# One weight quadrant of the gated feed-forward layer taken by a second level of Strassen: the upper right block of gate and up in a fused transformer layer

## The chip, the cores and the metric

The kernel runs on one core of a Trainium2 chip. The metric is the device time of one launch in microseconds; lower is better. The engines of the core are TensorE (PE, with its weight loads PEld), VectorE (DVE), ScalarE (ACT), GpSimd (POOL) and SyncE (SP), which only starts transfers here.

## The reference, cut to what matters

The program is a whole hybrid layer (latent attention, an RWKV branch, output projection, feed-forward) over 1024 prompt tokens and 32 sample tokens. The change touches its last part alone:

```
def layer_tail(x, attn, rw, attn_out_g, w_out, norm_ffn_g, w_gate, w_up, w_down):
    mix = jnp.concatenate([rmsnorm(attn, attn_out_g), rw], axis=-1)
    h = x + mix @ w_out
    u = rmsnorm(h, norm_ffn_g)
    return h + (jax.nn.silu(u @ w_gate) * (u @ w_up)) @ w_down
```

All is float32. The model width is 1024 (8 blocks of 128, `KD`), the hidden width 2816 (22 blocks, `FB`), and there are 1056 tokens (`TOK`).

## The kernel before, in words

The function is `tail`. Tokens lie along the free dimension; `uT` holds the normed input as 8 depth blocks by 1056 tokens. The products with gate and up are done by Strassen's scheme in Winograd's form with seven products: the weights are cut in two row blocks (output block `pair` and `pair + 11`) and two depth halves of four blocks (`KH`), the tokens in two halves of 528, and each half in two column quarters of 264 (`NW`). A **unit** is one matrix (gate or up) and one pair of output blocks: 22 units, even ones gate, odd ones up. A unit has two **steps**, one for each column quarter `nh`: 44 steps.

A step computes, in PSUM banks X, Y, Z, W (banks 0 to 3 in even steps, 4 to 7 in odd ones), in this order: X = A11·B11, Y = S2·T2, Z = S3·B12, W = S1·T1, and then on top of what the banks hold X += A12·B21, Z += A22·T4, W += S4·B22. Each product is four matmuls of 128x264, and each float32 matmul is two records in the trace, so a product is 8 records. Between them ScalarE copies the first content of X into `p1_`, and VectorE adds it through the others: `u2 = Y + P1` (line 2910), `u3 = Z + u2` (2912), `u3 = W + u3` (2914). The second product of X waits for the copy, that of Z for 2912, that of W for 2914. After these, VectorE finishes the four output quadrants. In gate steps (lines 2921 to 2938) it multiplies by the row factors `rb`, ScalarE takes a tanh, and VectorE writes (1 + tanh)·value into `hid`; in up steps (2940 to 2948) it multiplies `hid` by half the result. All are VectorE operations of 128x264; some read one operand from PSUM and one from SBUF, the others read both from SBUF (2921, 2927, 2928, 2933 to 2940, 2947, 2948).

GpSimd makes the four weight sums of each unit, 128x512 each (S1, S2, S3, S4; lines 2795, 2797, 2798, 2800), from the weights that SyncE loads into the two buffers `ab[0]` (gate) and `ab[1]` (up), 2 x 512 KB each unit. The load of a unit waits until the unit that used its buffer is through (line 2505).

After the units come eight steps of the down projection (`DOWN`) of the same form, with products of eleven matmuls and weight sums by GpSimd (lines 2805 to 2819); its token sums (`sums`, lines 2960 to 2966) are VectorE's. Its first step needs the first weights `Alo` (in the gate buffer) and `Ahi` (in the up buffer).

The order of all work on each engine is written out by hand; the engines meet by semaphores alone.

Of the kernel before, what the change touches and what calls it, by code (L numbers as in the profile page):

```python
# [11 lines left out]
P = 128  # L12
# [2397 lines left out]
def tail(nc, g, io, phase):  # L2410
# [26 lines left out]
    wa = [w[:, :, :] for w in g.wo] + slots[0:4]  # L2437
# [6 lines left out]
    p1_ = [sb(f"p1_{i}", [P, NW]) for i in range(2)]  # L2444
# [8 lines left out]
    sw = [w[:, 2 * KD * P:].rearrange("p (s k n) -> p s k n", s=3, k=KH) for w in wA]  # L2453

# [10 lines left out]
    names = """xr_in0 xr_in1 xr_in2 xr_in3 xr_in4 xr_in5 xr_in6 xr_in7 g_in hi_in5 hi_in6 hi_in7 in0 in1 in2 in3 lo_read u_hi1 zero ps_done end_done part_ok h_ok hc_ok sq_ok acc_ok ssq_ps ms_ok r_ok rb_ps rb_ok u_lo u_hi h_st  # L2465
# [7 lines left out]
    UNITS = 2 * FH  # L2473
    DOWN = [(nh, j) for nh in range(2) for j in range(KH)]

    @block.sync
    def _(sp):
# [34 lines left out]
        for u in range(2, UNITS):  # L2512
            sp.wait_ge(s["w_ps"], 2 * u - 2)
            load_unit(u)

        def rows(j):
            return io.w_down[j]

        for n, (nh, j) in enumerate(DOWN):
            sp.wait_ge(s["w_ps"], 2 * UNITS - 2)  # L2520
            if n:
# [3 lines left out]
            sp.dma_start(Alo[:, 0:FH], rows(j)[:, 0:FH]).then_inc(s["a11_in"], 16)  # L2525
            if n == 0:
                sp.dma_start(Alo[:, FH:], rows(j)[:, FH:]).then_inc(s["a12_in"], 16)
            sp.wait_ge(s["w_ps"], 2 * UNITS)
# [34 lines left out]
    def _(pe):  # L2563
# [53 lines left out]

        for u in range(UNITS):
            b = u % 2
            pe.wait_ge(s[f"w_in{b}"], 32 * (u // 2 + 1))  # L2620
            for nh in range(2):
                it, c = 2 * u + nh, slice(nh * NW, nh * NW + NW)
                X, Y, Z, W = (4 * (it % 2) + i for i in range(4))
                half = lambda t: (lambda k: t[:, k, c])
                left = lambda w: (lambda k: w[:, k, :])
                A11, A12, S3, A22 = (ab[b][:, a, KH * d:KH * d + KH] for a in range(2) for d in range(2))
                if it == 0:
                    pe.wait_ge(s["hc_ok"], KD - 2)
                    pe.wait_ge(s["u_lo"], KH)
                if it == 1:  # L2630
                    pe.wait_ge(s["h_ok"], 2 * KD)
                    pe.wait_ge(s["hc_ok"], KD)
                if it >= 2:
                    pe.wait_ge(s["x_done"], it - 1)
                product(X, left(A11), half(B11u), KH, "p1_ps")
                if it == 1:
                    row_factors()
                if it == 0:
                    pe.wait_ge(s["s1_ok"], 1)
                    pe.wait_ge(s["t1_ok"], 1)  # L2640
                    product(W, left(sw[b][:, 0]), half(T1u), KH, "p5_ps")
                pe.wait_ge(s["s2_ok"], u + 1)
                if it == 0:
                    pe.wait_ge(s["t2_ok"], 1)
                if it == 1:
                    pe.wait_ge(s["rb_ok"], 1)
                if it >= 2:
                    pe.wait_ge(s["y_done"], it - 1)
                product(Y, left(sw[b][:, 1]), half(T2u), KH, "p6_ps")
                pe.wait_ge(s["s3_ok"], u + 1)  # L2650
                if it == 0:
                    pe.wait_ge(s["t3_ok"], 1)
                if it == 1:
                    pe.wait_ge(s["rb_ok"], 2)
                if it >= 2:
                    pe.wait_ge(s["z_done"], it - 1)
                product(Z, left(S3), half(B12u), KH, "p7_ps")
                if it == 0:
                    pe.wait_ge(s["u_hi"], KH)
                else:  # L2660
                    pe.wait_ge(s["s1_ok"], u + 1)
                    if it == 1:
                        pe.wait_ge(s["rb_ok"], 3)
                    if it >= 2:
                        pe.wait_ge(s["w_done"], it - 1)
                    product(W, left(sw[b][:, 0]), half(T1u), KH, "p5_ps")
                pe.wait_ge(s["p1_ok"], it + 1)
                product(X, left(A12), half(B21u), KH, "x_ps", first=False)
                if it == 0:
                    pe.wait_ge(s["t4_ok"], 1)  # L2670
                pe.wait_ge(s["u3_ok"], it + 1)
                product(Z, left(A22), half(T4u), KH, "z_ps", first=False)
                pe.wait_ge(s["s4_ok"], u + 1)
                pe.wait_ge(s["c22_ok"], it + 1)
                product(W, left(sw[b][:, 2]), half(B22u), KH, "w_ps", first=False)
                if it == 0:
                    row_sums()

        for n, (nh, j) in enumerate(DOWN):
            X, Y, Z, W = (4 * (n % 2) + i for i in range(4))  # L2680
# [3 lines left out]
            left = lambda w: (lambda k: w[:, k, :])  # L2684
            pe.wait_ge(s["a11_in"], 16 * n + 16)
            if n == 0:
                pe.wait_ge(s["hid_ok"], 6 * UNITS)
            if n >= 2:
                pe.wait_ge(s["q_x"], n - 1)
            product(X, left(Alo[:, 0:FH]), lo0, FH, "q1_ps")  # L2690
# [34 lines left out]
    def _(act):  # L2725
# [26 lines left out]
        for u in range(UNITS):  # L2752
            for nh in range(2):
                it = 2 * u + nh
                X, Y, Z, W = (4 * (it % 2) + i for i in range(4))
                act.wait_ge(s["p1_ps"], it + 1)
                act.activation(p1_[it % 2][:, :], pb[X][:, 0:NW], ACT.Copy).then_inc(s["p1_ok"], 1)  # L2757
                if it == 0:
                    for last in (KD - 2, KD - 1):
                        squares(last)  # L2760
                if u % 2:
                    continue
                n = u + nh + 1
                act.wait_ge(s["c22_s"], n)
                act.activation(th[1], part[1][:, :], ACT.Tanh, scale=0.5).then_inc(s["th22"], 1)
                act.wait_ge(s["c11_ok"], n)
                act.activation(th[0], g11[:, :], ACT.Tanh, scale=0.5).then_inc(s["th11"], 1)
                act.wait_ge(s["c21_ok"], n)
                act.activation(th[2], part[2][:, :], ACT.Tanh, scale=0.5).then_inc(s["th21"], 1)
                act.wait_ge(s["c12_ok"], n)  # L2770
                act.activation(th[3], part[0][:, :], ACT.Tanh, scale=0.5).then_inc(s["th12"], 1)
        for n in range(len(DOWN)):
            act.wait_ge(s["q1_ps"], n + 1)
            if n >= 2:
                act.wait_ge(s["q_u2"], n - 1)
            act.activation(p1_[n % 2][:, :], pb[4 * (n % 2)][:, 0:NW], ACT.Copy).then_inc(s["q1_ok"], 1)  # L2776

    @block.gpsimd
    def _(pool):
# [7 lines left out]
        for u in range(UNITS):  # L2787
            if u == 2:
                pool.wait_ge(s["ms_ok"], 2)
                tt(row_ms[:, :], row_ms[:, :], minus_half, ALU.pow).then_inc(s["r_ok"], 1)  # L2790
            b = u % 2
            A11, A12, A21, A22 = (ab[b][:, a, KH * d:KH * d + KH] for a in range(2) for d in range(2))
            S1, S2, S4 = (sw[b][:, i] for i in range(3))
# [4 lines left out]
            tt(A21, A11, A21, ALU.subtract).then_inc(s["s3_ok"], 1)  # L2798
            pool.wait_ge(s["s2_ok"], u + 1)
            tt(S4, A12, S2, ALU.subtract).then_inc(s["s4_ok"], 1)  # L2800
        pool.wait_ge(s["w_ps"], 2 * UNITS)
        for n in range(len(DOWN)):
            pool.wait_ge(s["a11_in"], 16 * n + 16)
# [18 lines left out]
    def _(dve):  # L2822
# [77 lines left out]
        for u in range(UNITS):  # L2900
            pair = u // 2
            if u == 2:
                dve.wait_ge(s["h_st"], 16)
            for nh in range(2):
                it = 2 * u + nh
# [9 lines left out]
                if it == 0:  # L2915
                    row_means()
                    row_factors()
# [206 lines left out]
```

## Time and profile before

| | |
|---|---|
| median of 3 runs | 1805.3 us (1804.81 to 1805.52) |
| the profiled execution's own time | 1805.66 us |
| its span, first to last instruction | 1803.9 us |
| mean granted TensorE clock | 0.992 |
| PE busy | 1728.3 us, 96% of the span |
| DVE busy | 951.5 us, 53% |
| ACT busy | 414.0 us, 23% |
| POOL busy | 617.5 us, 34% |

The span is one profiled execution; what is added to it in the profiled execution's own time, 1.8 us, lies around the first and last instruction. Busy time of PE counts matmuls from issue to modelled end, so neighbours overlap; how fast they follow each other is read from the timeline or from the chain of work that ended last.

### The profile page before, as it was taken

The page shows a single profiled execution, that of the slowest core. Times are in us where ns is not written, and L with a number is a line of the kernel's source. Part 1 is how long each engine was busy: PE and PEld are TensorE (multiplying, and loading weights), DVE is VectorE, ACT ScalarE, POOL GpSimd, SP SyncE. Part 2 cuts the span into 40 slices and gives each one's busy share as a digit, 9 for nine tenths or more (in the row PEclk, how much of TensorE's full clock was granted, in tenths as well). Part 3 has the DMA queues.
Part 4 walks back from the last instruction along what each step waited for, and adds up shares of the span by engine and source line. Part 5 has one row for each costly group of instructions (what it writes and reads, how often), then busy time and mean ns, then how long its engine had stood idle before and what let it go on. Part 6 is the DMA issues. An engine that isn't in the chain of part 4 may idle for free.

```text
span 1803.9 us, 34817 instructions
## 1 busy us (share of the span) xinstructions
PE 1728.3 (96%) x14732; PEld 1309.8 (73%) x14732; DVE 951.5 (53%) x1758; ACT 414.0 (23%) x945; POOL 617.5 (34%) x431
## 2 busy tenths in 40 slices
PE   5899999999998996999999999999999999999998
PEld 4566666666665654666666888888888888888887
DVE  2757767767766675666435433444433345526322
ACT  2343333333334232556211001011110010000000
POOL 2654663663653552000150211222212221635332
PEclk9999999999999998999999999999999999999999
DMA  9443253243244312610052111011110112333431
GB/s 351 161 159 109 62 163 109 78 146 109 79 134 112 106 40 73 184 49 13 18 223 96 47 47 47 25 47 47 48 47 24 47 47 76 121 104 105 145 104 53
DMA packets 89008, 169.36 MB, mean 94 GB/s; under 512 B 29627, under 2 KB 62987, under 8 KB 84630
## 3 DMA queue, kind: packets, MB, share of 16 engines
q1 hardware_dynamic: 79510, 117.85, 20.5%
q10 hardware_dynamic: 9344, 49.29, 7.9%
q8 instruction: 118, 1.93, 0.4%
q14 instruction: 36, 0.29, 0.1%
HBM read 136.40 MB, written 23.04 MB: 88 GB/s over the span
## 4 chain that ended last, share of the span: by engine, by line
PE 49%; DVE 1%; issue 0%; POOL 0%; ACT 0%; DVEq 0%
PE psum L2613 45%; PE psum L2566 4%; DVE u_sum L2876 0%; DVE mixT L2877 0%; PE psum L2601 0%; POOL row_ms L2790 0%; DVE mixT L2850 0%; DVE hid L2847 0%; DVE rb L2896 0%; PE psum L2607 0%; DVE hid L2837 0%; DVE yout L2997 0%; DVE part L2946 0%; DVE part L2996 0%; DVE part L2912 0%
## 5 line engine op out<-in xcount | busy, mean ns | idle before, releaser
L2613 PE MATMUL psum<-mixT,wA 128*128 128x264 f32 x1408 | 335.2, 386 | 0.4 <-DVE mixT L2877 0.4
L2613 PEld LDWEIGHTS psum<-mixT,wA 128*128 128x128 f32 x1408 | 267.4, 190 | 46.4 <-issue 0.8
L2613 PE MATMUL psum<-u_sum,wA 128*128 128x264 f32 x1232 | 297.2, 386 | 2.3 <-DVE part L2912 1.5
L497 PE MATMUL psum<-wsl,xt 128*128 128x368 f32 (+2 forms) x1100 | 286.4, 451 | 8.8 <-DMA wsl<-in_w_in 5.5
L2613 PEld LDWEIGHTS psum<-u_sum,wA 128*128 128x128 f32 x1232 | 233.8, 190 | 43.0 <-issue 3.2
L497 PEld LDWEIGHTS psum<-wsl,xt 128*128 128x128 f32 (+1 forms) x1100 | 151.8, 172 | 91.9 <-issue 18.1
L2795 POOL TENSOR_TENSOR wA<-wA 128x512 f32<-128x512 f32 x22 | 29.4, 1337 | 392.4 <-DMA wA<-in_w_gate 197.1
L2613 PE MATMUL psum<-hid,wA 128*128 128x264 f32 x528 | 120.2, 386 | 2.1 <-DVE hid L2948 1.5
L2613 PEld LDWEIGHTS psum<-hid,wA 128*128 128x128 f32 x528 | 100.2, 190 | 19.9 <-issue 2.8
L2201 PE MATMUL psum<-kT,qT 104*128 104x346 f32 (+7 forms) x224 | 80.1, 477 | 12.5 <-DMA kT<-scratch_kT 9.1
L1539 POOL TENSOR_TENSOR Ls<-Lraw,con 128x512 f32<-128x512 f32 x45 | 48.8, 1093 | 97.1 <-ACT Lraw L1143 66.1
L2613 PE MATMUL psum<-mixT,u_sum 128*128 128x264 f32 x352 | 79.8, 386 | 0.0
L2757 ACT ACTIVATE p<-psum 128x264 f32<-128x264 f32 x44 | 17.1, 390 | 253.6 <-PE psum L2613 253.4
L2613 PEld LDWEIGHTS psum<-mixT,u_sum 128*128 128x128 f32 x352 | 66.8, 190 | 11.7 <-POOL u_sum L2815 0.3
L1505 POOL TENSOR_TENSOR st<-st,con 128x3 f32<-128x3 f32 (+1 forms) x18 | 50.7, 2816 | 60.6 <-DVE st L1702 31.3
L1143 ACT ACTIVATE proj<-psum,rstd 128x368 f32<-128x368 f32 (+1 forms) x72 | 36.9, 512 | 142.9 <-PE psum L497 142.3
L2367 DVE TENSOR_REDUCE part<-psum 128x1 f32<-128x347 f32 (+5 forms) x88 | 44.3, 523 | 43.1 <-PE psum L2201 42.1
L2289 ACT ACTIVATE pq<-psum,neg 128x346 f32<-128x346 f32 (+7 forms) x112 | 59.8, 542 | 27.6 <-DVE neg L2370 21.4
L2805 POOL TENSOR_TENSOR wA<-wA 128x1408 f32<-128x1408 f32 x8 | 25.5, 3182 | 112.1 <-DMA wA<-in_w_down 112.1
L2776 ACT ACTIVATE p<-psum 128x264 f32<-128x264 f32 x8 | 3.1, 391 | 255.0 <-PE psum L2613 255.0
L2910 DVE TENSOR_TENSOR part<-psum,p 128x264 f32<-128x264 f32 x44 | 19.0, 432 | 79.2 <-PE psum L2613 79.1
L2341 POOL COPY wide<-rec 128x256 f32<-128x256 f32 x16 | 6.4, 402 | 154.4 <-DVE rec L2380 154.4
(363 smaller groups left out, 2904.0 us busy)
## 6 DMA issues: line engine op xcount, KB each, us to landing
wsl<-in_w_in ACTq DMA_DIRECT2D x27, 1472.0 KB, 6.5
wA<-in_w_down SPq DMA_DIRECT2D x32, 704.0 KB, 4.2
wA<-in_w_gate SPq DMA_DIRECT2D x22, 512.0 KB, 4.3
wA<-in_w_up SPq DMA_DIRECT2D x22, 512.0 KB, 4.3
mixed<-proj SPq DMA_DIRECT2D x8, 784.0 KB
xt<-in_x_tiles SPq DMA_DIRECT2D x9, 512.0 KB, 5.1
wsl<-in_w_in SPq DMA_DIRECT2D x3, 1472.0 KB, 13.4
hid<-in_x_cols SPq DMA_DIRECT2D x8, 528.0 KB, 7.2
```

The lines of the kernel that those rows point to most:

```text
L497: return pe.matmul(out, lhsT, rhs, start=start, stop=stop)
L1143: copy = lambda out, in_, **k: act.activation(out, in_, ACT.Copy, **k)
L1505: tt(out, ms, c_("minus_half")[:, 0:n], ALU.pow).then_inc(s[ok], 1)
L1539: tt(Ls[i % 2][:, :, :], Lraw[:, :, :], bcast(c_("levels")[:, i * 64:(i + 1) * 64], 1, H), ALU.mult).then_inc(s["Ls_ok"], 1)
L2201: pe.matmul(pb[n % BANKS][:, 0:y - x], qT[b][0:ROWS, t * P:(t + 1) * P], kT[b][0:ROWS, x:y], start=True, stop=True).then_inc(s["s_ps"], 1)
L2289: act.activation(rows_of(a, t)[:, x:y], pb[n % BANKS][:, 0:y - x], ACT.Exp, bias=neg[:, i % RINGS:i % RINGS + 1], accum_out=sums[:, pair % ...
L2367: dve.tensor_reduce(part[:, r, u:u + 1], src, AX.X, ALU.max).then_inc(s["part_ok"], 1)
L2566: last = pe.matmul(pb[bank][:, 0:c.stop - c.start], w[:, k, :], g.mixT[:, first_k + k, c], start=start and k == 0, stop=stop and k == 3, s ...
L2613: ins = pe.matmul(pb[bank][:, 0:NW], left(k), right(k), start=first and k == 0, stop=k == depth - 1, skip_group_check=not first)
L2795: tt(S1, A21, A22, ALU.add).then_inc(s["s1_ok"], 1)
L2805: tt(Ahi[:, 0:FH], Alo[:, 0:FH], Ahi[:, 0:FH], ALU.subtract).then_inc(s["e3_ok"], 1)
L2910: named(tt(u2, Y, p1_[it % 2][:, :], ALU.add), "y_done", it + 1)
```

## The change

The product A12·B21 (upper right weight block, four depth blocks) is no longer part of the seven products of each step. A step of first level keeps six products; its first content of X is only copied. Two units (four steps) form a **double**: the two weight blocks A12 of the double's two units are taken as two row blocks, their four depth blocks as two halves of two (`DK`), the two column quarters of B21 as the two column blocks, and their product, the same that four first-level steps used to need, is done by a further step with seven products of two matmuls each (`second_level`). There are 11 doubles of 5 steps, 55 steps in all. The first double mixes gate and up of the last block pair; the others are two gate units, then two up units of the same two blocks, in turn.

The copies P1 of the four first-level steps are kept in four buffers until the second-level step adds its results to them: VectorE then has per double 17 operations in the second-level step of a gate double, 13 in that of an up double, 15 in the mixed one; a first-level step has 11 (gate) or 8 (up) where it had 13 or 9. GpSimd gets four sums of 128x256 per double, VectorE four sums of 128x528 once, after the second step. The weights are loaded in other pieces and at other moments: A11 with the second row block (256 and 512 KB) as before, but the second unit's only after the fourth step of the double before, and the A12 blocks (256 KB each) after its second-level step. GpSimd's order in a double is S1, S2, S3 of the first unit, S1, S2, S3 of the second, S4 of both, then the four small sums. At the start of the down projection the first weights come in three pieces, one of which (`Alo[:, KH:2*KH]`, which lies where A12 of the first unit is) is loaded only after the last step, and the matmuls of the first product are put in another order.

```
+    DOUBLES = [((0, FH - 1), (1, FH - 1))] + [((b, p), (b, p + 1)) for p in range(0, FH - 1, 2) for b in range(2)]
+    STEPS = [(d, j) for d in range(FH) for j in range(5)]
...
-        for u in range(2, UNITS):
-            sp.wait_ge(s["w_ps"], 2 * u - 2)
-            load_unit(u)
+        for d in range(1, FH):
+            sp.wait_ge(s["w_ps"], 5 * d - 3)
+            load_unit(2 * d)
+            sp.wait_ge(s["w_ps"], 5 * d - 1)
+            load_unit(2 * d + 1)
+            sp.wait_ge(s["w_ps"], 5 * d)
+            load_twelve(2 * d)
+            load_twelve(2 * d + 1)
...
         for n, (nh, j) in enumerate(DOWN):
-            sp.wait_ge(s["w_ps"], 2 * UNITS - 2)
+            if n == 0:
+                sp.wait_ge(s["w_ps"], N_STEPS - 3)
+                sp.dma_start(Alo[:, 0:KH], rows(j)[:, 0:KH]).then_inc(s["lo_in"], 16)
+                sp.dma_start(Alo[:, 2 * KH:FH], rows(j)[:, 2 * KH:FH]).then_inc(s["lo_in"], 16)
+                sp.dma_start(Alo[:, FH:], rows(j)[:, FH:]).then_inc(s["a12_in"], 16)
+                sp.wait_ge(s["w_ps"], N_STEPS)
+                sp.dma_start(Alo[:, KH:2 * KH], rows(j)[:, KH:2 * KH]).then_inc(s["a11_in"], 16)
...
-                product(X, left(A12), half(B21u), KH, "x_ps", first=False)
...
+        def second_level(it, d):
+            X, Y, Z, W = (4 * (it % 2) + i for i in range(4))
+            pe.wait_ge(s["p1_ok"], it - 1)
+            for b in range(2):
+                pe.wait_ge(s[f"w12_in{b}"], 16 * (d + 1))
+            product(X, left(a11), left(b11), DK, "p1_ps")
+            pe.wait_ge(s["d2_ok"], d + 1)
+            pe.wait_ge(s["dt4_ok"], 1)
+            pe.wait_ge(s["y_done"], it - 1)
+            product(Y, left(d2), left(t2), DK, "p6_ps")
+            pe.wait_ge(s["d3_ok"], d + 1)
+            pe.wait_ge(s["z_done"], it - 1)
+            product(Z, left(a21), left(b12), DK, "p7_ps")
+            pe.wait_ge(s["d1_ok"], d + 1)
+            pe.wait_ge(s["w_done"], it - 1)
+            product(W, left(d1), left(t1), DK, "p5_ps")
+            pe.wait_ge(s["p1_ok"], it + 1)
+            product(X, left(a12), left(b21), DK, "x_ps", first=False)
+            pe.wait_ge(s["u3_ok"], it + 1)
+            product(Z, left(a22), left(t4), DK, "z_ps", first=False)
+            pe.wait_ge(s["d4_ok"], d + 1)
+            pe.wait_ge(s["c22_ok"], it + 1)
+            product(W, left(d4), left(b22), DK, "w_ps", first=False)
...
+            if n == 0:
+                pe.wait_ge(s["lo_in"], 32)
+                pe.wait_ge(s["hid_ok"], 16 * FH - 4)
+                order = [0, 1, 2, 3, 10, 4, 5, 6, 7, 8, 9]
...
+        for it, (d, j) in enumerate(STEPS):
+            X, kind = 4 * (it % 2), double_kind(d)
+            if d and j == 0:
+                act.wait_ge(s["x_done"], d)
+            if d and j == 1:
+                act.wait_ge(s["fold_ok"], 3 * d)
+            act.wait_ge(s["p1_ps"], it + 1)
+            act.activation(p1_[j], pb[X][:, 0:NW], ACT.Copy).then_inc(s["p1_ok"], 1)
...
+        for d in range(FH):
...
+                three_sums(2 * d)
+                three_sums(2 * d + 1)
+                fourth_sum(2 * d)
+                fourth_sum(2 * d + 1)
+            pool.wait_ge(s["s4_ok"], 2 * d + 2)
+            tt(d1, a21, a22, ALU.add).then_inc(s["d1_ok"], 1)
+            pool.wait_ge(s["d1_ok"], d + 1)
+            tt(d2, d1, a11, ALU.subtract).then_inc(s["d2_ok"], 1)
+            tt(a21, a11, a21, ALU.subtract).then_inc(s["d3_ok"], 1)
+            pool.wait_ge(s["d2_ok"], d + 1)
+            tt(d4, a12, d2, ALU.subtract).then_inc(s["d4_ok"], 1)
...
+        def second_sums():
+            dve.wait_ge(s["t4_ok"], 1)
+            named(tt(t1, b12, b11, ALU.subtract), "dt1_ok", 1)
+            named(tt(t2, b22, t1, ALU.subtract), "dt2_ok", 1)
+            tt(b12, b22, b12, ALU.subtract).then_inc(s["dt3_ok"], 1)
+            tt(t4, b21, t2, ALU.subtract).then_inc(s["dt4_ok"], 1)
...
+        def second_level(it, d):
...
+            front(it, X, Y, Z, W, p1_[4])
+            named(tt(u3, u3, p1_[3], ALU.add), "fold_ok", 3 * d + 1)
+            if kind == GATES:
+                n_gate += 1
+                named(tt(u3, u3, r1, ALU.mult), "c22_s", n_gate)
+            elif kind == UPS:
+                stt(odd1, odd1, 0.5, u3, ALU.mult, ALU.mult).then_inc(s["hid_ok"], 1)
+            dve.wait_ge(s["x_ps"], d + 1)
+            named(tt(g11[:, :], X, p1_[0], ALU.add), "x_done", d + 1)
...
+            dve.wait_ge(s["z_ps"], it + 1)
+            named(tt(c21, Z, u2, ALU.add), "z_done", it + 1)
+            named(tt(c21, c21, p1_[2], ALU.add), "fold_ok", 3 * d + 2)
...
+            dve.wait_ge(s["w_ps"], it + 1)
+            named(tt(u2, W, u2, ALU.add), "w_done", it + 1)
+            named(tt(u2, u2, p1_[1], ALU.add), "fold_ok", 3 * d + 3)
```

`front` is the three additions of lines 2910, 2912 and 2914 of the kernel before.

## Rows read from the trace of the kernel before

**Rows 1.** The page's first lines: span, busy time of two engines
```profile
span 1803.9 us, 34817 instructions
PE 1728.3 (96%) x14732; PEld 1309.8 (73%) x14732; DVE 951.5 (53%) x1758; ACT 414.0 (23%) x945; POOL 617.5 (34%) x431
```

**Rows 2.** The chain that ended last, in order of time: start, duration, work
```profile
987.76 534.25 PE psum L2613 x2400
...
1523.50 5.15 PE psum L2613 x22
...
1529.20 269.63 PE psum L2613 x1210
```

**Rows 3.** Busy time by stage: the start of gate and up, and its bulk
```profile
966.00:988.00 22.00, 19.02 (x95) 15.24 (x94) 14.26 (x17) 4.95 (x7) 1.79 (x1) 1.00 0.49 197
988.00:1522.00 534.00, 534.00 (x2400) 455.65 (x2399) 213.94 (x480) 53.82 (x131) 103.67 (x80) 1.00 0.12 43
```

**Rows 4.** Timeline of the first step (start, duration, engine, line)
```profile
973.05 3.80 PE L2613 MATMUL psum<-mixT,wA 128*128 128x264 f32 x16 [0.37 <-DVE mixT L2877]
...
977.77 0.43 DVE L2912 TENSOR_TENSOR part<-psum,part 128x264 f32<-128x264 f32 x1
...
978.35 2.02 PE L2613 MATMUL psum<-u_sum,wA 128*128 128x264 f32 x8 [1.50 <-DVE part L2912]
```

**Rows 5.** Timeline where a gate unit ends and an up unit begins
```profile
1046.58 3.72 PE L2613 MATMUL psum<-mixT,wA 128*128 128x264 f32 x16
...
1048.63 0.43 DVE L2930 TENSOR_TENSOR part<-psum,part 128x264 f32<-128x264 f32 x1 [0.61 <-PE psum L2613]
...
1050.36 0.43 DVE L2938 SCALAR_TENSOR_TENSOR hid<-yout,part 128x264 f32<-128x264 f32 x1
```

**Rows 6.** Timeline of VectorE and GpSimd, one meeting of the two
```profile
1030.83 0.43 DVE L2914 TENSOR_TENSOR part<-psum,part 128x264 f32<-128x264 f32 x1 [1.35 <-PE psum L2613]
1031.29 1.33 DVE L2921 TENSOR_TENSOR part<-part,rb 128x264 f32<-128x264 f32 x1
...
1031.06 1.27 POOL L2797 TENSOR_TENSOR wA<-wA 128x512 f32<-128x512 f32 x1
1032.29 1.46 POOL L2798 TENSOR_TENSOR wA<-wA 128x512 f32<-128x512 f32 x1
```

**Rows 7.** Timeline: first and last of 20 unit loads, GpSimd's first sum after each
```profile
998.71 0.80 SPq L2505 DMA_DIRECT2D wA<-in_w_gate  x2
...
1005.19 1.27 POOL L2795 TENSOR_TENSOR wA<-wA 128x512 f32<-128x512 f32 x1 [19.01 <-DMA wA<-in_w_gate]
...
1472.19 0.80 SPq L2505 DMA_DIRECT2D wA<-in_w_up  x2
...
1476.88 1.27 POOL L2795 TENSOR_TENSOR wA<-wA 128x512 f32<-128x512 f32 x1 [19.39 <-DMA wA<-in_w_up]
```

**Rows 8.** Timeline of the passage into the down projection
```profile
1522.03 0.33 SPq L2532 DMA_DIRECT2D wA<-in_w_down  x1
...
1526.31 3.27 POOL L2805 TENSOR_TENSOR wA<-wA 128x1408 f32<-128x1408 f32 x1 [44.16 <-DMA wA<-in_w_down]
1526.60 6.02 DVE L2961 TENSOR_TENSOR mixT<-hid 128x2904 f32<-128x2904 f32 x1
...
1544.01 0.96 PEld L2613 LDWEIGHTS psum<-mixT,u_sum 128*128 128x128 f32 x5 [0.31 <-POOL u_sum L2815]
```

**Rows 9.** The page's costliest groups: a GpSimd sum of 1408 columns (busy us, mean ns)
```profile
L2805 POOL TENSOR_TENSOR wA<-wA 128x1408 f32<-128x1408 f32 x8 | 25.5, 3182 | 112.1 <-DMA wA<-in_w_down 112.1
```

**Rows 10.** DMA issues by line: a transfer of 256 KB
```profile
proj<-in_w_out ACTq DMA_DIRECT2D x7, 256.0 KB, 3.0
```

**Rows 11.** Busy time by stage around TensorE's longest pause
```profile
706.00:716.00 10.00, 0.52 (x6) 0.32 (x4) 1.31 (x4) 0.68 (x2) 2.98 (x18) 0.69 0.40 106
716.00:726.00 10.00, 6.90 (x13) 4.20 (x14) 2.45 (x6) 2.07 (x8) 0.00 (x0) 0.50 0.66 144
726.00:736.00 10.00, 9.69 (x52) 6.63 (x51) 7.76 (x17) 6.70 (x22) 0.00 (x0) 0.95 1.09 273
```

More of the change, by code:

```diff
@@ L2616, in product @@
             return ins
[L2618 to L2629, printed above, removed]
+        left = lambda w: (lambda k: w[:, k, :])
@@ new lines, in first_level @@
+        def first_level(it, d, j):
+            b, nh = j // 2, j % 2
+            c = slice(nh * NW, nh * NW + NW)
+            X, Y, Z, W = (4 * (it % 2) + i for i in range(4))
+            half = lambda t: (lambda k: t[:, k, c])
+            A11, _, S3, A22 = (ab[b][:, a, KH * x:KH * x + KH] for a in range(2) for x in range(2))
+            u = 2 * d + b
+            pe.wait_ge(s[f"w_in{b}"], 32 * (d + 1))
+            if it == 0:
+                pe.wait_ge(s["hc_ok"], KD - 2)
+                pe.wait_ge(s["u_lo"], KH)
+            if it == 1:
+                pe.wait_ge(s["h_ok"], 2 * KD)
+                pe.wait_ge(s["hc_ok"], KD)
+            if it >= 2:
+                pe.wait_ge(s["p1_ok"], it - 1)
+            if d and j == 1:
+                pe.wait_ge(s["x_done"], d)
+            product(X, left(A11), half(B11u), KH, "p1_ps")
+            if it == 1:
+                row_factors()
+            if it == 0:
+                pe.wait_ge(s["s1_ok"], 1)
+                pe.wait_ge(s["t1_ok"], 1)
+                product(W, left(sw[b][:, 0]), half(T1u), KH, "p5_ps")
+            pe.wait_ge(s["s2_ok"], u + 1)
+            if it == 0:
+                pe.wait_ge(s["t2_ok"], 1)
+            if it == 1:
+                pe.wait_ge(s["rb_ok"], 1)
+            if it >= 2:
+                pe.wait_ge(s["y_done"], it - 1)
+            product(Y, left(sw[b][:, 1]), half(T2u), KH, "p6_ps")
+            pe.wait_ge(s["s3_ok"], u + 1)
+            if it == 0:
+                pe.wait_ge(s["t3_ok"], 1)
+            if it == 1:
+                pe.wait_ge(s["rb_ok"], 2)
+            if it >= 2:
+                pe.wait_ge(s["z_done"], it - 1)
+            product(Z, left(S3), half(B12u), KH, "p7_ps")
+            if it:
+                pe.wait_ge(s["s1_ok"], u + 1)
@@ L2630, in _ @@
                 if it == 1:
-                    pe.wait_ge(s["h_ok"], 2 * KD)
-                    pe.wait_ge(s["hc_ok"], KD)
+                    pe.wait_ge(s["rb_ok"], 3)
                 if it >= 2:
[L2634 to L2666, printed above, removed]
@@ L2667, in _ @@
-                pe.wait_ge(s["p1_ok"], it + 1)
-                product(X, left(A12), half(B21u), KH, "x_ps", first=False)
[L2669 to L2675, printed above, removed]
@@ L2676, in _ @@
-                if it == 0:
-                    row_sums()
+                    pe.wait_ge(s["w_done"], it - 1)
+                product(W, left(sw[b][:, 0]), half(T1u), KH, "p5_ps")
+            if it == 0:
+                pe.wait_ge(s["t4_ok"], 1)
+            pe.wait_ge(s["u3_ok"], it + 1)
+            product(Z, left(A22), half(T4u), KH, "z_ps", first=False)
+            pe.wait_ge(s["s4_ok"], u + 1)
+            pe.wait_ge(s["c22_ok"], it + 1)
+            product(W, left(sw[b][:, 2]), half(B22u), KH, "w_ps", first=False)
@@ L2683, in _ @@
             hi0, hi1 = (lambda k: hid[:, FH + k, c0]), (lambda k: hid[:, FH + k, c1])
-            left = lambda w: (lambda k: w[:, k, :])
-            pe.wait_ge(s["a11_in"], 16 * n + 16)
             if n == 0:
[L2687 to L2690, printed above, removed]
+                pe.wait_ge(s["lo_in"], 32)
+                pe.wait_ge(s["hid_ok"], 16 * FH - 4)
+                order = [0, 1, 2, 3, 10, 4, 5, 6, 7, 8, 9]
+                for k in order:
+                    if k == 4:
+                        pe.wait_ge(s["a11_in"], 16)
+                    elif k == 8:
+                        pe.wait_ge(s["hid_ok"], 16 * FH)
+                    last = pe.matmul(pb[X][:, 0:NW], Alo[:, k, :], lo0(k), start=k == order[0], stop=k == order[-1])
+                last.then_inc(s["q1_ps"], 1)
+            else:
+                pe.wait_ge(s["a11_in"], 16 * n + 16)
+                if n >= 2:
+                    pe.wait_ge(s["q_x"], n - 1)
+                product(X, left(Alo[:, 0:FH]), lo0, FH, "q1_ps")
             def x_close():
@@ L2751, in _ @@
             weighted(k, slice(0, HT), "u_hi")
[L2752 to L2771, printed above, removed]
+        halved = lambda out, in_: act.activation(out, in_, ACT.Tanh, scale=0.5)
@@ L2952, in _ @@
+        u2, u3, c21 = (x[:, :] for x in part)
+        for it, (d, j) in enumerate(STEPS):
+            if d == 1 and j == 0:
+                dve.wait_ge(s["h_st"], 16)
+            if j < 4:
+                first_level(it, d, j)
+            else:
+                second_level(it, d)
+            if it == 1:
+                second_sums()
+        dve.wait_ge(s["w_ps"], N_STEPS)
         for n, (nh, j) in enumerate(DOWN):
```

251 lines of the change are left out of this document (174 added, 77 removed).

## The prediction

> **What bounds the kernel now.** I read the page first: PE is busy for 96% of the span, and DVE and POOL for 53% and 34% [rows 1]. Busy time alone doesn't tell that an engine sets the pace, so the chain that ended last comes next: from 987.76 us it is one run of 2400 matmul records, 534.25 us without a pause, then the passage into the down projection, then 1210 records in 269.63 us [rows 2]. A record thus takes 534.25 / 2400 = 0.2226 us, and 269.63 / 1210 = 0.2228 us where products are 22 records long instead of 8: the border between two products costs nothing. A product of four matmuls (8 records) takes 1.78 us, one of two matmuls 0.89 us. In the bulk of gate and up DVE works 214 and POOL 104 of 534 us [rows 3]. They look idle; what matters is when their work falls and whether it meets.
>
> **What the change takes away.** Before, a double's four steps have 4 x 28 = 112 matmuls; after, 4 x 24 + 14 = 110. Over 11 doubles 22 matmuls, 44 records, go: 44 x 0.2226 = 9.8 us. Not all of it is won. In the first step TensorE already waits 1.50 us for line 2912 before the second product of Z [rows 4], and nothing ahead of 2912 on VectorE gets shorter. Without the product A12·B21 it reaches that wait 1.78 us earlier and leaves it at the same time (978.35). So 8.0 us remain.
>
> **Waits inside the steps, if VectorE runs undisturbed.** Delays from the timeline: VectorE starts 0.27 us after the last record of its product has been issued (W's second product 1046.58 to 1048.36, line 2930 at 1048.63 [rows 5]); an operation takes 0.43 us, a dependent next one starts 0.03 us later; TensorE starts 0.14 us after VectorE ends (2912 ends at 978.20, matmul at 978.35 [rows 4]). In a first-level step, counted from its start, Z ends at 5.34, 2912 gives its result at 5.34 + 0.27 + 0.43 + 0.14 = 6.18, and Z's second product wants it at 7.12; for W it is 7.96 against 8.90. In the second-level step: Z ends at 2.67, result at 3.51, wanted at 4.45; W 4.40 against 5.34. ScalarE's copy of X, behind the last tanh of the step before (about 1.6), is there at about 2.2, wanted at 3.56. So a slack of 0.9 us, and no wait. The 103 more VectorE operations (587 against 484, about 44 us), 11 copies on ScalarE and 44 sums of 128x256 on GpSimd lie beside matmuls by total time. Such a sum: (3.18 - 1.27) / 896 columns = 2.13 ns a column from the two shapes, 1.27 us being the undisturbed one [rows 6, 9], so 0.73 us. The four sums of 128x528 after step 2 take about 0.7 us each (my estimate from 0.43 us at 264 columns and one cycle of the same slope, 1.0 ns a column, up to 2904 columns in 3.0 us), 2.9 in all; VectorE is then ready about 5.0 us into step 3, u2 and u3 can follow before 7.12. Costed at nothing; if they met GpSimd's sums, up to 0.5 us once.
>
> **Where the work meets.** In [rows 6] line 2914, which reads PSUM and SBUF, takes 0.43 us while GpSimd runs. Line 2921, both operands in SBUF, starts at 1031.29 inside GpSimd's sum of 1031.06 to 1032.33 and takes 1.33 us: it ends 0.29 us after that sum. I looked at all VectorE operations of the bulk with two SBUF operands that start while GpSimd works: 20 operations, 0.45 to 1.47 us long, all end 0.28 to 0.30 us after the end of a GpSimd sum. The next sum gives way in turn (1.46 instead of 1.27 us). With long operands it is plainer: the 2904 columns of line 2961, issued at 1526.60, last 6.02 us, where GpSimd's 1526.31 + 3.27 leaves them 3.03 us [rows 8]. So the two engines alternate, one whole instruction each. The Trainium skill has the sharing (GPSIMD Engine Reference, Key points: SBUF interfaces shared with VectorE, contention with instructions that have two SBUF inputs), and the trace agrees; that it goes by whole instructions is from the rows.
>
> Before, this costs nothing: GpSimd's four sums start 4.7 to 6.5 us after the unit's load is issued (first pair 6.48, last 4.69, median of 20 pairs 4.84 [rows 7]) and meet one or two such operations in the middle of a step. After the change, look at the end of a second-level step (E). The second unit's load is issued 6.0 us before E. It is 768 KB instead of 1024, at some 0.38 MB/us 0.6 us less, so GpSimd starts S1 4.2 us after it, at E - 1.9. From there GpSimd has S1, S2, S3, S4, S4 and four small sums nearly without a pause (the two A12 blocks are issued at E + 0.2 and land 3.0 us later [rows 10], when S3 is just over). Exactly then VectorE has the longest series of two-SBUF operations in the kernel. Gate double, ends in us from E, VectorE's operation after the GpSimd sum that holds it:
> S1 -0.4, row factor on u3 -0.1; (X + P1, PSUM, 0.4); S2 1.0, row factor 1.3; (Z + u2, PSUM, 1.8); S3 2.5, add P1 2.75; row factor 3.2, in the gap before the A12 block; S4 4.35, gate product 4.6; (W + u2, PSUM, 5.0); S4 5.8, add P1 6.1; small sum 6.65, row factor 6.9; 7.5, product 7.8; 8.4, product 8.7; 9.3, product 9.6. Then 2910 and 2912 of the next step: 10.0 and 10.5, TensorE goes on at 10.6. It wanted this at 7.12. **A wait of 3.5 us in each gate double.** Undisturbed, the same series ends at E + 4.2 (before: 2.4 us after the last product [rows 5]) and waits for nothing.
>
> For later or earlier landing (S1 at E - 2.2 to E - 0.3) the same count gives 3.0 to 3.9 us; I take 3.4. In the mixed double there are seven such operations after E: 2912 at E + 8.6, wait 1.4 to 2.5, I take 1.7. In an up double four; VectorE is free by about E + 5.5 and the wait is 0 to 0.7 us; I take 0. Five gate doubles and one mixed: 5 x 3.4 + 1.7 = 18.7 us. The wait moves all later work as a whole and is not won back: TensorE has no other slack.
>
> **Into the down projection.** Before, TensorE waits 1.5 us for VectorE, and later 0.3 us for GpSimd's sum behind line 2815 [rows 8], 22.0 us after the last product: transfer of `Ahi` 4.3 us, then 17.7 us of sums that alternate with VectorE. After, the first five matmuls run at once, then TensorE waits for 256 KB issued at the end (3.0 us [rows 10]): it is about 0.5 us ahead of before at the second product. But `Ahi` is issued 0.4 us later and behind those 256 KB, so it lands 0.4 to 1.2 us later, and the sums with it. Net loss 0.4 to 1.2, I take 0.7 us.
>
> **Sum.** -9.8 + 1.8 + 18.7 + 0.7 = +11.4 us on the profiled 1803.9 us span and 1805.66 us own time, which is 0.36 us over the median of the runs; on that: 1805.3 + 11.4 = 1816.7 us. Changes under 0.2% (3.6 us) count as same; this is about what a measurement of this kernel can tell from no change.
>
> **Rivals.** (1) The meeting is milder: either the sums come at another time or VectorE gets its operations between them, all waits hide. Then -8.0 + 0.7 = -7.3: 1798.0 us, faster. For it: the slacks above are 0.9 us and more, and total VectorE load is about half; against it: 20 of 20 operations behave alike, and GpSimd's series begins by the landing of a load whose issue is fixed to the fourth step's end. It decides where the gate doubles' wait falls under 0.7 us. A wait of 1.1 to 2.4 us each (-7.3 + 5.5 x 1.1 to 2.0) gives 1799 to 1809, mostly "same".
> (2) The clock falls in the new waits. After its longest pause, 9 us, TensorE was granted 0.50 for 716 to 726 [rows 11], the 1.2 GHz level, and was back at 0.95 of 2.4 GHz in the next ten: some 7.3 us of matmuls at half rate, 3.7 us lost. If each of five waits did this: +18.4, 1835 us. Against it: with pauses of 1.5 and 2.6 us the stretch 966 to 988 stayed at 1.00 [rows 3]. The Trainium skill (TensorE: Matmul & The Clock Gate, the section on why this matters for your kernels) advises against pauses above some 3 us between bursts, which would bring the clock down here; the rows here hold no pause between 2.6 and 9 us that would decide it.
> (3) Borders of short products cost something: 77 products of 4 records, at 0.05 us each +3.9 us; the rows for 8 and 22 records show none. Taken at 0, kept in the upper end.
>
> **How the numbers follow.** The alternation with waits of 2.4 to 4.5 us in gate doubles 0.76; milder, about no change 0.06; all hidden 0.12; the clock falls as well 0.06. Range: from waits of 1.5 us in the gate doubles and 0.8 in the mixed one (1798.0 + 8.3 = 1806.3) to 4.5, 2.4 and four times 0.7 (1798.0 + 27.7 = 1825.7), 1806 to 1826; outside lie the hidden case and the falling clock. Slower 0.82, same 0.06, faster 0.12.
>
> **What would show it.** 3652 records of line 2613's successor instead of 3696. In gate doubles the product Z += A22·T4 of the step behind the second-level step starts 3 to 4 us late, released by VectorE's u3; five such pauses, one smaller, none (or under 0.7) behind up doubles. VectorE's two-SBUF operations there take 0.7 to 1.4 us instead of 0.43, ending 0.29 us after a GpSimd sum. S1 of the double's second unit starts 1 to 2 us before the second-level step ends. The prediction is wrong if those operations stay at 0.43 us, if GpSimd's sums start several us later, or if the granted clock leaves 1.00.

## The result: 24 us slower, and what the profile shows

The changed kernel takes 1829.5 us (median of 4 runs, 1827.8 to 1831.6) against 1805.4 us: ratio 1.0132, 95% interval 1.0119 to 1.0144. The sign and the place were forecast; 1829.5 lies outside the range of 1806 to 1826, and the change is twice the forecast one (+24.1 against +11.4 us).

The page of the changed kernel, its first lines:
```profile
span 1827.3 us, 35060 instructions
PE 1733.0 (95%) x14688; PEld 1308.2 (72%) x14688; DVE 1029.2 (56%) x1861; ACT 417.4 (23%) x956; POOL 655.5 (36%) x475
```
There are 44 matmul records fewer, and 103 VectorE and 44 GpSimd instructions more, than in [rows 1], as counted. The chain of work that ended last is no longer one piece of TensorE. This is its part behind the second gate double (start, duration, work):
```profile
1178.65 1.39 DVE part L3076
1180.06 0.44 DVE g L3080
1180.53 0.93 DVE g L3085
1181.48 0.45 DVE part L3087
1181.95 0.93 DVE part L3088
1182.91 0.44 DVE part L3092
1183.37 1.39 DVE hid L3094
...
1185.14 1.05 DVE part L3097
1186.21 0.85 DVE part L3102
1187.09 0.74 DVE hid L3104
1187.85 0.95 DVE hid L3107
1188.79 0.80 DVE hid L3109
1189.62 0.44 DVE part L3023
1190.08 0.44 DVE part L3025
1190.57 89.84 PE psum L2647 x396
```
These are VectorE's operations of the second-level step and the first two additions of the next step, back to back; those that read PSUM (3080, 3087, 3023, 3025) take 0.44 us, those with two SBUF operands mostly 0.74 to 1.39 (3092, in a gap of GpSimd's series, 0.44). TensorE waits for the last of them; that is the first loss. Then 396 records take 89.84 us; at 0.2226 us each [rows 2] they would take 88.15. That is the second loss.

The timeline shows the meeting itself, behind the first gate double, whose last product ends at 1076.46:
```profile
1074.80 1.28 POOL L2879 TENSOR_TENSOR wA<-wA 128x512 f32<-128x512 f32 x1 [17.55 <-DMA wA<-in_w_up]
1074.99 1.39 DVE L3076 TENSOR_TENSOR part<-part,rb 128x264 f32<-128x264 f32 x1
1076.16 1.35 POOL L2881 TENSOR_TENSOR wA<-wA 128x512 f32<-128x512 f32 x1
...
1079.38 2.86 POOL L2888 TENSOR_TENSOR wA<-wA 128x512 f32<-128x512 f32 x2 [0.44 <-DMA wA<-in_w_up]
...
1079.73 1.38 DVE L3094 SCALAR_TENSOR_TENSOR hid<-yout,part 128x264 f32<-128x264 f32 x1
...
1082.32 0.80 POOL L2904 TENSOR_TENSOR con<-wA 128x256 f32<-128x256 f32 x1
1082.57 0.84 DVE L3102 TENSOR_TENSOR part<-part,rb 128x264 f32<-128x264 f32 x1
...
1086.93 3.19 PE L2647 MATMUL psum<-u_sum,wA 128*128 128x264 f32 x8 [3.19 <-DVE part L3025]
```
Line 3076 waits for the sum of 1074.80 to 1076.08 and ends 0.30 us behind it; 3102 does the same with a small sum (1083.12 and 1083.41). From 994 to 1545 us every VectorE operation with two SBUF operands that starts during a GpSimd sum does so: 87 of 87 end 0.29 to 0.30 us behind it, and take up to 1.55 us. The last line holds both losses: TensorE was idle for 3.19 us ahead of it, released by u3 (line 3025), and its 8 records take 3.19 us, where [rows 5] has 16 in 3.72.

Who waited for whom on TensorE, 994 to 1545 us (us in total, times, longest):
```profile
PE psum L2647 <- DVE part L3025: 18.2, 7, 3.3
```
Seven waits: 1.93 us behind the mixed double, 3.19, 3.18, 3.18, 3.27, 3.17 behind the gate doubles, one of 0.34 behind an up double. The first step's wait went from 1.50 [rows 4] to 3.29 us, as forecast. All idle pauses of TensorE between 966 us and the fourth product of the down projection sum to 25.8 us, before to 5.0; each pause costs some 0.17 us more than its listed length, because it is counted from the modelled end of the matmul before it (behind the first gate double the records are 3.35 us further apart than usual, where 3.19 is listed).

The granted clock, in stretches of 12 us: the first step, then behind the five gate doubles. The columns are the stretch, its length, the busy time (and count) of PE, PEld, DVE, ACT and POOL, the granted clock as a share of 2.4 GHz, the DMA share and GB/s; the last number but two is the clock:
```profile
976.00:988.00 12.00, 10.42 (x51) 8.60 (x51) 3.43 (x8) 1.08 (x1) 2.90 (x3) 0.86 0.14 57
1084.00:1096.00 12.00, 9.07 (x33) 7.53 (x34) 5.31 (x11) 0.54 (x2) 1.65 (x2) 0.86 0.00 0
1188.00:1200.00 12.00, 9.43 (x36) 7.88 (x37) 5.39 (x11) 0.39 (x1) 1.29 (x2) 0.86 0.01 2
1291.00:1303.00 12.00, 9.63 (x30) 7.78 (x31) 4.75 (x10) 0.39 (x1) 1.09 (x2) 0.72 0.00 1
1395.00:1407.00 12.00, 9.25 (x34) 7.67 (x35) 5.17 (x12) 0.39 (x1) 1.47 (x2) 0.86 0.00 0
1498.00:1510.00 12.00, 9.07 (x34) 7.51 (x35) 5.31 (x11) 0.54 (x2) 1.65 (x2) 0.86 0.01 1
```
Before, the same stage had 1.00 throughout [rows 3]. In shorter stretches the value is 0.50, the 1.2 GHz level, and soon 1.00 again:
```profile
1088.00:1090.00 2.00, 2.00 (x6) 1.49 (x6) 0.00 (x0) 0.00 (x0) 0.00 (x0) 0.50 0.00 0
1090.00:1092.00 2.00, 2.00 (x8) 1.66 (x7) 0.43 (x1) 0.00 (x0) 0.00 (x0) 0.73 0.00 0
1092.00:1094.00 2.00, 2.00 (x10) 1.71 (x10) 1.21 (x3) 0.00 (x0) 0.00 (x0) 1.00 0.00 0
```
TensorE works through the slow part, so what is missing to 1.00, times 12 us, is the time that it lost: five times 1.7 and once 3.4 (1291 to 1303), 11.8 us.

The balance of the profiled executions: -9.8 (records) + 20.7 (pauses) + 1.4 (eight more of them, 0.17 each) + 11.8 (clock) = 24.1; the stage began 1.05 us earlier than in the execution of the kernel before, which leaves 23.1 of the 23.4 us by which the spans differ.

### The profile page after: what moved, and what is told of

It reads as the page before. It is cut to its first block, busy times and chain, and to the rows that moved or that the text cites. A ratio compares the mean times of both kernels' runs of the same rounds, so it can differ in the third digit from the quotient of the medians.

```text
span 1827.3 us, 35060 instructions
## 1 busy us (share of the span) xinstructions
PE 1733.0 (95%) x14688; PEld 1308.2 (72%) x14688; DVE 1029.2 (56%) x1861; ACT 417.4 (23%) x956; POOL 655.5 (36%) x475
## 3 DMA queue, kind: packets, MB, share of 16 engines
q8 instruction: 118, 1.93, 0.4%
## 4 chain that ended last, share of the span: by engine, by line
PE 44%; DVE 5%; POOL 1%; issue 0%; DMA 0%; SPq 0%; DVEq 0%; POOLq 0%
PE psum L2647 40%; PE psum L2600 4%; DVE part L3097 0%; DVE hid L3094 0%; DVE part L3088 0%; DVE g L3085 0%; POOL u_sum L2921 0%; POOL u_sum L2925 0%; DVE hid L3109 0%; DVE hid L3104 0%; DVE part L3076 0%; DVE hid L3107 0%; DVE part L3102 0%; DMA wA<-in_w_down 0%; DVE part L3092 0%
## 5 line engine op out<-in xcount | busy, mean ns | idle before, releaser
L2647 PE MATMUL psum<-mixT,wA 128*128 128x264 f32 x1188 | 287.6, 389 | 0.4 <-DVE mixT L2988 0.4
L2647 PEld LDWEIGHTS psum<-u_sum,wA 128*128 128x128 f32 x1232 | 237.7, 194 | 68.3 <-DVE part L3025 22.3
L2647 PEld LDWEIGHTS psum<-mixT,wA 128*128 128x128 f32 x1188 | 228.4, 192 | 40.8 <-issue 0.8
L2647 PE MATMUL psum<-hid,wA 128*128 128x264 f32 x506 | 115.1, 386 | 0.6 <-ACT p L2863 0.6
L2647 PEld LDWEIGHTS psum<-hid,wA 128*128 128x128 f32 x506 | 96.1, 190 | 17.3 <-issue 1.0
L2824 ACT ACTIVATE yout<-part 128x264 f32<-128x264 f32 x82 | 34.7, 423 | 241.0 <-DVE part L3042 136.4
L2863 ACT ACTIVATE p<-psum 128x264 f32<-128x264 f32 x8 | 3.1, 391 | 250.5 <-PE psum L2647 239.8
L2201 PEld LDWEIGHTS psum<-kT,qT 104*128 104x128 f32 x224 | 38.4, 194 | 26.4 <-issue 17.4
```

The costliest lines, as they stand in the source:

```text
L2201: pe.matmul(pb[n % BANKS][:, 0:y - x], qT[b][0:ROWS, t * P:(t + 1) * P], kT[b][0:ROWS, x:y], start=True, stop=True).then_inc(s["s_ps"], 1)
L2647: ins = pe.matmul(pb[bank][:, 0:NW], left(k), right(k), start=first and k == 0, stop=k == depth - 1, skip_group_check=not first)
L2824: halved = lambda out, in_: act.activation(out, in_, ACT.Tanh, scale=0.5)
```

## Experiments

Eight kernels in two sets. Each set has its own runs of the kernel before: 1806.4 us (14 runs) beside the sums held back, the small sums later, the wait filled and the first step filled, 1806.2 us (13 runs) beside the other four. The first four told here ask whether waits and clock are what they seem, and which is whose. The recorded expectations call the kernel with the sums held back e1_sums_held, or e1.

**Sums held back.** GpSimd begins the series only when VectorE is past u3 of the double's first step; the first unit's fourth sum also moves to its head:
```
             else:
                 three_sums(2 * d)
-                three_sums(2 * d + 1)
-                fourth_sum(2 * d)
+                pool.wait_ge(s["u3_ok"], 5 * d + 1)
+                fourth_sum(2 * d)
+                three_sums(2 * d + 1)
                 fourth_sum(2 * d + 1)
```

> The changed kernel with one order altered on GpSimd: in every double but the first it waits for line 3025's sum (u3) of the double's first step before S4 of the first unit and all that follows; no work is left out. Theory A (the waits come from GpSimd's sums alternating with VectorE's operations behind the second-level step, and the clock falls in these waits): the waits of 3.2, 1.9 and 0.3 us go, the granted clock stays 1.00 from 994 us on, and of the 24 us five clock losses of 2.2 us, 18.3 us of waits go: 1829.5 - 29 = about 1799 to 1801 us. Rival B (VectorE's longer series alone makes the wait, GpSimd is a bystander): the waits stay above 2 us and the time above 1820 us. Rival C (holding the sums back makes S4 or the small sums late, a new wait in front of W += S4*B22 or in the second-level step): 1 us or more in each double, 1810 us or above.

1799.4 us (5 runs), 30 us under the changed kernel; against the kernel before 0.9967, 0.9954 to 0.9980, so a third of a percent faster, clear of the interval. Its bulk and its chain:
```profile
1000.00:1500.00 500.00, 500.00 (x2249) 426.96 (x2248) 261.26 (x542) 52.89 (x133) 132.78 (x120) 1.00 0.13 43
```
```profile
991.90 520.93 PE psum L2647 x2340
...
1513.22 4.32 DMA wA<-in_w_down
```
The bulk is 2340 records in one piece, 0.2226 us each: no wait, no fall of the clock, and 110 matmuls in a double cost what 110 matmuls cost. Behind the first gate double, whose last product now ends at 1072.10, the row factor that took 1.39 us (line 3076 there, 3077 here) is one of the undisturbed operations, and GpSimd's series starts 6.1 us behind that end:
```profile
1070.64 0.43 DVE L3077 TENSOR_TENSOR part<-part,rb 128x264 f32<-128x264 f32 x1
...
1078.23 1.27 POOL L2888 TENSOR_TENSOR wA<-wA 128x512 f32<-128x512 f32 x1 [25.25 <-DVE part L3026]
```
The small sums come late for nobody. Theory A holds; B and C are out: the longer series alone makes no wait, and there is no new one.

**Small sums later.** Only the four small sums wait:
```
             pool.wait_ge(s["s4_ok"], 2 * d + 2)
+            if d:
+                pool.wait_ge(s["u3_ok"], 5 * d + 1)
             tt(d1, a21, a22, ALU.add).then_inc(s["d1_ok"], 1)
```

> The changed kernel; only the four small GpSimd sums (128x256) of a double wait for u3 of its first step, S1 to S4 stay where they are; no work is left out. Theory A: four of the operations behind the second-level step run undisturbed (0.43 instead of 0.8 to 1.0 us), so the wait in gate doubles falls from 3.2 to 1.6 us, that of the mixed double from 1.9 to about 1.0. A wait of 1.6 us leaves the clock at 1.00 (as 1.9 us did behind the mixed double): 5 x 1.6 + 1 + 0.3 of waits and 11 us of clock less, 1808 to 1811 us. Rival D (the clock falls at any wait of this size in this stage): 1818 to 1821 us. Rival B (GpSimd is a bystander): unchanged, 1829 us.

1811.5 us (8 runs), just above A's 1808 to 1811. The waits:
```profile
PE psum L2647 <- DVE part L3027: 8.5, 6, 2.0
```
1.40, 1.39, 1.98, 1.41 and 1.83 us behind the gate doubles, 0.53 behind the mixed one. The clock stayed at 1.00 behind all of them, here behind the first four gate doubles:
```profile
1040.00:1400.00 360.00, 353.83 (x1585) 300.41 (x1585) 192.13 (x384) 39.05 (x97) 94.98 (x84) 1.00 0.13 42
```
So the wait grows with the number of sums that VectorE meets, and a pause of half the length was not only half as dear here: it spared the clock.

**Wait filled.** Six matmuls without use ahead of the wait, in the five steps behind gate doubles:
```
+            if j == 0 and d and double_kind(d - 1) == GATES:
+                pe.wait_ge(s["p1_ok"], it + 1)
+                for k in range(6):
+                    pe.matmul(pb[X][:, 0:NW], A22[:, k % KH, :], T1u[:, k % KH, c], start=k == 0, stop=k == 6 - 1)
             if it == 0:
                 pe.wait_ge(s["t4_ok"], 1)
             pe.wait_ge(s["u3_ok"], it + 1)
```

> The changed kernel with six more matmuls (12 records, 2.67 us) on TensorE in the first step behind each of the five gate doubles, ahead of the wait for u3, into a PSUM bank whose content has been copied already; their result is not used. The waits for u3 stay, but TensorE works through most of them: remaining idle 0.5 us. Theory A with the clock as a cost of its own: the granted clock stays 1.00 there, u3 comes at the same time, and the five losses of about 2.2 us go: 1817 to 1820 us. Rival E (the 13 us that records and waits don't explain are not the clock but something else in these steps, or the added matmuls only lengthen the step): 1829 us or more.

1821.0 us (4 runs): thirty matmuls more and 8.5 us less than the changed kernel. VectorE and GpSimd meet as in the changed kernel (here line 3098 takes 1.38 us as 3094 did), u3 comes as late (10.4 us behind the double's last product in both), and TensorE is granted the full clock:
```profile
1072.00:1100.00 28.00, 27.55 (x124) 23.09 (x123) 18.48 (x32) 3.49 (x9) 10.20 (x9) 1.00 0.15 47
```
The clock is thus a cost of its own: in the profiled execution of the changed kernel the five falls behind gate doubles lost 10.1 us, and 8.5 us came back. The time is 1 us above the forecast; in the first step, which this kernel leaves as it is, the clock still fell.

**A wait without the meeting.** To the kernel with the sums held back, one wait is added on TensorE, on a GpSimd result that comes late by itself:
```
+            if j == 0 and d and double_kind(d - 1) == GATES:
+                pe.wait_ge(s["s2_ok"], 2 * d + 2)
             pe.wait_ge(s["u3_ok"], it + 1)
             product(Z, left(A22), half(T4u), KH, "z_ps", first=False)
```

> The kernel of e1_sums_held, in which GpSimd and VectorE do not meet behind the second-level step, with one wait more on TensorE: in the first step behind each of the five gate doubles, ahead of Z += A22*T4, it waits for GpSimd's S2 of the double's second unit, about 3.0 us longer than it would. Theory A (the loss is wait plus clock, whatever makes TensorE wait): five waits of 2.9 to 3.2 us, and the granted clock falls to 0.5 behind most of them, 1.7 us each: 20 to 25 us over e1, 1819 to 1825 us. Rival F (the clock falls because of what VectorE and GpSimd do together, not because TensorE stands still): the clock stays 1.00, 15 us over e1, 1814 to 1815 us. Rival G (a wait just under that of the changed kernel is short enough): also 1814 to 1815 us, with the waits read at 2.9 us.

1823.0 us (4 runs), 23.6 over the kernel it was made from. The waits and the five stretches behind them:
```profile
PE psum L2647 <- POOL wA L2883: 14.3, 5, 3.1
```
```profile
1084.00:1096.00 12.00, 9.21 (x34) 7.30 (x33) 3.11 (x6) 0.39 (x1) 8.24 (x9) 0.86 0.01 1
1187.00:1199.00 12.00, 8.86 (x27) 7.09 (x27) 3.47 (x6) 0.08 (x1) 8.18 (x9) 0.72 0.01 2
1291.00:1303.00 12.00, 9.21 (x34) 7.28 (x33) 3.12 (x6) 0.39 (x1) 8.21 (x9) 0.86 0.00 0
1393.00:1405.00 12.00, 9.21 (x34) 7.31 (x33) 3.11 (x6) 0.39 (x1) 8.85 (x9) 0.86 0.01 1
1496.00:1508.00 12.00, 9.21 (x34) 7.25 (x34) 3.12 (x6) 0.39 (x1) 8.50 (x9) 0.86 0.00 1
```
Pauses of 2.79 us four times and 3.14 once, VectorE undisturbed behind the second-level step, and the clock falls behind all five: 15 us of pauses and 10 of clock, about the 23.6 measured. Rivals F and G are out: VectorE and GpSimd need not meet for the clock to fall, and 2.79 us was not short enough.

**Smaller edits on the kernel with the sums held back.** Seven matmuls without use in the first step's wait (the line of the experiment above with `it == 0`):

> The kernel of e1_sums_held with seven more matmuls (3.1 us) in the very first step ahead of its wait of 3.3 us for u3, into a bank already copied; their result is not used. Theory A: that wait is no longer idle, the clock does not fall there (in the changed kernel it falls after 977 us), and the time is 1.7 to 2.2 us under e1. Rival: the fall in the first step is hidden by the row factors that follow, no difference to e1 beyond 0.5 us.

1800.1 us (6 runs), no difference to 1799.4 that could be told. The profiled executions don't decide it either: with the sums held back the clock did not fall behind the first step's pause of 3.29 us, though it fell behind the same pause in the changed kernel, so there was nothing to win. From the first pause on T1 to the last on the row factors both take 17.1 us, the changed kernel 18.8; a fall there is thus not hidden by the row factors. The spans of the two executions differ by 4.1 us, and all of it lies ahead of this stage. How often the clock falls in the first step in the executions without a profile is not known.

VectorE's squares behind the three additions:
```
-        add_squares(KD - 2)
 
         def row_means():
+            add_squares(KD - 2)
             add_squares(KD - 1)
```

> The kernel of e1_sums_held; VectorE adds the seventh block's squares (1.26 us) behind the three additions of the first step instead of ahead of them. Theory A: the wait in the first step falls from 3.3 to 2.0 us, the squares make the row sums about 0.6 us late, so 0.7 us are won, and where the clock fell in the first step in e1's executions another 1.7 us: 0.7 to 2.4 us under e1 (1797 to 1798.7), with the stage from 966 to the row factors 0.7 us shorter. Rival: the chain of the squares ends last in any case, no gain.

1801.0 us (6 runs), again no difference. The pause did shrink, from 3.29 to 1.99 us, and a new one of 0.43 behind the squares appeared; but here the clock fell as well (0.95 over 966 to 1000), so the stretch took 17.6 us. It fell later than in the changed kernel, some 6 us behind the end of the longer pause and 2 us behind that of the shorter one:
```profile
976.00:982.00 6.00, 4.82 (x25) 3.98 (x26) 3.52 (x5) 1.08 (x1) 0.00 (x0) 1.00 0.42 165
982.00:984.00 2.00, 2.00 (x13) 1.85 (x13) 0.22 (x2) 0.00 (x0) 0.47 (x1) 0.72 0.00 0
```
16 records of products lie between the two pauses, and 18 records of one column each behind the second; which of these brought the clock down is not shown. Against 18.8 for a first step with a falling clock it is a gain, against 17.1 for one without it is none.

The second weights of the down projection sooner:
```
+                sp.wait_ge(s["w_ps"], N_STEPS - 1)
+                sp.dma_start(Ahi[:, 0:KH], rows(j + KH)[:, 0:KH]).then_inc(s["hi_lo_in"], 16)
+                sp.dma_start(Ahi[:, 2 * KH:FH], rows(j + KH)[:, 2 * KH:FH]).then_inc(s["hi_lo_in"], 16)
+                sp.dma_start(Ahi[:, FH:], rows(j + KH)[:, FH:]).then_inc(s["a22_in"], 16)
                 sp.wait_ge(s["w_ps"], N_STEPS)
                 sp.dma_start(Alo[:, KH:2 * KH], rows(j)[:, KH:2 * KH]).then_inc(s["a11_in"], 16)
+                sp.dma_start(Ahi[:, KH:2 * KH], rows(j + KH)[:, KH:2 * KH]).then_inc(s["a21_in"], 16)
```

> The kernel of e1_sums_held; at the end of gate and up all of Ahi except the blocks that lie where A12 of the second unit is (256 KB) is loaded after the last first-level step instead of after the last step. Theory: GpSimd's sums of the down projection begin when 256 + 256 KB have landed instead of 256 + 704 + 704, about 1.1 us sooner, and the pause of 1.3 us before the product with S1 shrinks to 0.2 to 0.3 us: 1.0 to 1.2 us under e1. Rival: the sums wait for VectorE's sums of 2904 columns anyway (both alternate), so the pause stays at 1.3 us.

1800.5 us (5 runs). The rival was right. GpSimd's first sum starts 3.5 us after the last step's end instead of 4.9, and ends no earlier, because VectorE's first token sum holds it:
```profile
1519.57 3.18 DVE L3142 TENSOR_TENSOR hid<-hid 128x2904 f32<-128x2904 f32 x1
```
```profile
1520.88 4.89 POOL L2921 TENSOR_TENSOR wA<-wA 128x1408 f32<-128x1408 f32 x1 [37.12 <-DMA wA<-in_w_down]
```
It took 4.89 us instead of 3.54, and from the first issue at the end of the steps to the fourth product it is 22.8 us with and without the edit. So in these two executions the alternation of the two engines sets the passage, not the transfer.

All three edits together:

> The edits of e1, e5 and e6 together, no work left out. If the three causes are separate: 1.7 to 3.6 us under e1, 1796 to 1798 us, 8 to 10 us under the kernel before.

1800.2 us (6 runs), ratio to the kernel before 0.9969 (0.9958 to 0.9981). The clock fell in its first step too, again long (6.6 us) behind the pause of 2.00 us. The small edits add nothing that can be measured; the order of GpSimd's sums is all of the gain over the changed kernel. Among these kernels differences under 2 us stay open: in their single profiled executions the stages ahead of the feed-forward alone differ, with the pause on T1 between 969 and 975 us, and the later three were run beside the second set, not beside the kernel that they were made from.

## Why the prediction was wrong

**Right, with its sizes.** The matmuls saved: the kernel with the sums held back is 7.0 us faster than the one before; forecast for "all waits hide" was -7.3. The first step gives back 1.8 us: its pause grew by 1.79. The second-level step has no wait inside. VectorE and GpSimd alternate by whole instructions: forecast waits behind gate doubles 3.4 us, measured 3.2 listed and 3.36 with the 0.17; behind the mixed double 1.7, measured 1.9; behind up doubles 0, measured 0.34 once. Waits together 18.7 forecast, 18.2 listed. Both the experiment that takes the meeting away and the one that takes half of it away came out by this count. Passage into the down projection: the wait for the first weights 0.56, that for GpSimd's sum 1.62 us instead of 0.31, that for VectorE of 1.5 gone, about the 0.7 us forecast; its cause, though, is more the alternation than the transfer. One sum beside the main one is off: in rival (1) waits of 1.1 to 2.0 us give 1804 to 1809 us, not 1799 to 1809.

**Where it failed.** The step is rival (2), "the clock falls in the new waits", which was left out of the sum and given a chance of 0.06. It fell behind every new pause of 3.2 us and behind the first step's: 11.8 us that the sum of +11.4 did not have. Of the rival's own numbers the price was too high (3.7 us a fall, read where the matmuls behind a pause of 9 us were slow for longer; here 1.7, once 3.4) and the count too low (five; the first step's longer pause, which the prediction had worked out, is a sixth).

**What should have told.** The argument against the rival was a stretch with pauses of 1.5 and 2.6 us at full clock [rows 3], and that is a misreading. TensorE's idle time in that stretch is 22.00 - 19.02 = 2.98 us in all, and its pauses are 0.55, 0.37, 1.50, 0.28 and 0.27 us. The only 2.6 us there is VectorE's wait for TensorE:
```profile
986.92 1.38 DVE L2896 COPY rb<-psum 128x512 f32<-128x512 f32 x3 [2.62 <-PE psum L2607]
```
The prediction also says that its rows hold no pause between 2.6 and 9 us. The trace of the kernel before holds one of 3.79 us, in an earlier stage, and the clock fell there; 0.72 over 12 us is 3.4 us missing:
```profile
560.34 0.90 PE L589 MATMUL psum<-con,lat 128*128 128x128 f32 x3 [3.79 <-DVE lat L1712]
```
```profile
558.00:570.00 12.00, 9.06 (x117) 5.92 (x117) 7.86 (x18) 4.18 (x8) 2.47 (x3) 0.72 1.00 276
```
The same pause brought the clock down in all ten profiled executions. Pauses forecast at 3.0 to 3.9 us thus lay beside one with a fall and far from the 1.50 without, and a chance of 0.06 had no ground.

The advice of the Trainium skill (TensorE: Matmul & The Clock Gate, why this matters for your kernels) against pauses above some 3 us was quoted and not followed. The trace agrees for the pauses in question: the clock fell behind all ten pauses of 2.8 to 3.3 us behind gate doubles (the changed kernel and the one with the added wait) and behind none of the five of 1.4 to 2.0 us in the kernel with the small sums later. But the length alone does not decide. The first step's pause of 3.3 us brought the clock down in five profiled executions of six (not with the sums held back). Near the kernel's start, at 40 to 43 us, a pause of 1.83 us was followed by a fall in six profiled executions of ten. What separates these is not shown.

## What to carry to other kernels

Before work is added to an engine that looks half idle, lay its longest series beside the other engine's series on the same time axis: here VectorE operations with two SBUF operands and GpSimd sums took turns by whole instructions, and an operation of 0.43 us cost up to 1.55 beside sums of 1.3 to 1.5. Such a meeting can be mended by order alone: one wait that starts GpSimd's series some 8 us later, with one sum moved to its head, turned 24 us of loss into 7 us of gain. And a forecast pause of TensorE has two prices, its length and the slow records behind it; if it comes near the shortest pause that the trace shows with a falling clock, put both into the sum. Look for that pause in the whole trace, not only in the stage that changes, and check whose idle time a listed pause is.

## What the runs showed of the hardware

A pause of 1.4 us and one of 3.2 us differ by more than their length: in these steps the first cost 1.6 us, the second 3.4 and 1.7 of clock (once 3.4). Filling the pauses with matmuls whose result is not used was worth 8.5 us over five places, though VectorE's result came as late as before. GpSimd is held as VectorE is: a sum of 1408 columns took 4.89 us instead of 3.2 [rows 9] beside a VectorE operation of 2904 columns.
